# The last transposes of a stage moved among the next stage's early products, and a first stage that loads one weight piece ahead of the input

## The chip, the cores and the metric

The kernel runs on one core of a Trainium2 chip. The metric is the device time of one execution in microseconds (us). A core has a matrix engine, TensorE (PE in the profile; its weight loads are PEld), a vector engine, VectorE (DVE), a scalar engine, ScalarE (ACT), GpSimd (POOL) and SyncE (SP), which issues nearly all DMAs here. The engines run their own instruction streams and meet by semaphores.

## The reference, cut to what matters

The reference computes two blocks over 512 tokens of width 1024, in float32. `x` is (512, 1024).

```python
# block one, layer l in (0, 1); layer 0 has a dense feed-forward, layer 1 eight experts (top 2)
p = h @ w_in[l]                       # (512, 3888), then four sequence mixers on column groups
h = layer_norm(ALPHA * h + mixed @ w_out[l], ln1_g[l], ln1_b[l])
h = layer_norm(ALPHA * h + swiglu_or_experts(h), ln2_g[l], ln2_b[l])
# block two
x = x + 0.5 * rms_norm(swiglu(rms_norm(x, pre1), w_gu1, w_down1), post1)
x = x + rms_norm(hybrid_mixer(rms_norm(x, pre_mix), w_in_2, ...) @ w_o, post_mix)
x = x + 0.5 * rms_norm(swiglu(rms_norm(x, pre2), w_gu2, w_down2), post2)
```

What matters for the change: each big product needs its input feature by feature (features on the 128 partitions), while normalisation is done token by token. So between two products every tile of 128 tokens is transposed.

## The kernel before

**Products in three parts.** A float32 operand is held as two parts: a rounded one, made by ScalarE with a copy into a rounding type (`x_split` part 0, `w_split` part 0), and the rest, made by VectorE as the difference (part 1). A product is then three matmuls: rounded times rounded, and two mixed ones. `XR` (`x_split` in the profile) holds the transposed input, both parts.

**Stages.** The program is a row of stages. Each is a block in which every engine has its stream, and at whose end all engines meet; a stage starts when the last of them has arrived. Within a stage order is that of the code.

**The first stages.** `stage_load` issues the DMAs of the input (2 MB, one DMA), of four sets of constants, and of the first two weight pieces (256 columns of `w_in`, 1 MB each), and ends when the input and the constants are in. `stage_to_feature` transposes the whole input: 32 transposes of 128x128, and for each of 8 feature tiles a rounding on ScalarE and a rest on VectorE. Then `stage_stream` is the projection of layer 0: for every weight piece a rounding (1024 or 2048 elements a partition) on ScalarE, a rest on VectorE, and 48 matmuls of 512 columns on TensorE.

**Early products.** Later stages of this kind begin with a part of their first weight piece already multiplied. An `Early` object loads and splits that piece in the stage before. A `HeadStart` object runs its products for the first half of the tokens (columns 0 to 255 of `XR`) at the end of the stage before: `pe_first_tokens` waits until the piece is split and token tiles 0 and 1 are split (`moved.at(4)`), then runs 2 units (`u`) of 24 matmuls of 256 columns. `pe_last_tokens` runs the other 48 at the start of the next stage. There are four such joints: the end of `MixOut` in layer 0 (projection out of the mixers, into the dense feed-forward), the end of `LayerTail` (that feed-forward into the projection of layer 1), the end of `RootTail` (first feed-forward of block two into its projection) and the end of `OutTail`, a subclass of it (into the second feed-forward).

**The turning of a tile.** `pe_turn(t)` transposes token tile `t` in 8 transposes into two PSUM banks, `act_turned(t)` rounds them on ScalarE, and `dve_rests(t)` makes the rests on VectorE, each in two halves. The code at the end of a tail puts the early products before the last turning:

```python
if t == TT - 1 and self.start is not None:
    self.start.pe_first_tokens(self.moved.at(4), self.bank_free())
self.pe_turn(t)
```

In `RootTail` and `OutTail` the turnings run one tile later than in `LayerTail` (`behind` is 2), so that the turning of tile 2 stands in `pe_end` too. `dve_pre_norm(t)` makes the normalised rows (`h_tok`) for which `pe_turn(t)` waits.

Of the kernel before, what the change touches and what calls it, by code (L numbers as in the profile page):

```python
# [227 lines left out]
class HeadStart:  # L228
# [7 lines left out]

    def products(self, u, tokens, out=None):
        k, out = self.k, self.k.bank(self.banks[u]) if out is None else out
        for d in range(DT):
            trio = ((0, 0), (0, 1), (1, 0))  # L240
            for q, (i, j) in enumerate(trio):
                mm = self.nc.tensor.matmul(out[:, tokens], self.weights(u, i, d), k.XR[:, j, d, tokens], start=d == 0 and q == 0, stop=d == DT - 1 and q == 2)  # L242
        return mm

    def pe_first_tokens(self, split, free):
        pe = self.nc.tensor
        pe.wait_ge(*self.k.sig("early_rounded_part").at(1))
        pe.wait_ge(*self.k.sig("early_rest").at(1))
        pe.wait_ge(*split)
        pe.wait_ge(*free)  # L250
        for u in range(2):
            self.products(u, slice(0, SEQ // 2))

# [534 lines left out]
class RwkvFront(Part):  # L788
# [23 lines left out]
    def bank(self, b, n=HALF):  # L812
        return self.k.PS[:, R_PS + b * HALF:R_PS + b * HALF + n]
# [901 lines left out]
class RowTail(Part):  # L1715
# [146 lines left out]
class RootTail(RowTail):  # L1862
# [14 lines left out]
    def banks_free(self, pe):  # L1877
        pe.wait_ge(*self.first_sq.at(TT))

    def bank_free(self):  # L1880
# [79 lines left out]
    def dve_tile(self, t):  # L1960
        nc, s, k = self.nc, self.dve, self.k
        y, bank, r = k.H[:, t, :], self.scratch(t), self.col(self.r, t)
        self.dve_add(t)
        if t > 0 and self.pre:
            self.dve_new_variance(t - 1)
        nc.vector.wait_ge(*self.added.at(t + 1))
        s(nc.vector.tensor_tensor(bank, self.half(y, 1), self.half(self.gain, 1), ALU.mult))
        nc.vector.wait_ge(*self.second_sq.at(t + 1))
        nc.vector.tensor_scalar(r, self.col(self.second_sum, t), self.col(self.first_sum, t), D * RMS_EPS, ALU.add, ALU.add).then_inc(*self.var.up())
        if t > 0 and self.pre:  # L1970
            self.dve_new_factor(t - 1)
# [76 lines left out]
class MixOut(Part):  # L2048
# [160 lines left out]
    def pe_second_half(self):  # L2209
# [13 lines left out]
        if self.start is not None:  # L2223
            self.start.pe_first_tokens(self.moved.at(self.OWN + 4), self.added.at(TT + 2))
        self.pe_turn(last)
        if router is not None:
            self.pe_route(last)
# [68 lines left out]
class Kernel:  # L2296
# [386 lines left out]

    def stage_load(self, ahead):

        nc, ap = self.nc, self.ap
        loaded = self.sig("inputs_loaded")
        with nc.Block() as block:
            @block.sync
            def _(sp):  # L2690
                sp.dma_start(self.H, ap["x"][0].rearrange("(t p) d -> p t d", p=P)).then_inc(*loaded.up(16))
                sp.dma_start(self.CF[:, :], ap["const_f"]).then_inc(*loaded.up(16))
# [3 lines left out]
                ahead(sp)  # L2696
                sp.wait_ge(*loaded.at(80))

            @block.vector
            def _(dve):  # L2700
                dve.wait_ge(*loaded.at(80))
                for l in range(2):
# [3 lines left out]
        self.close()  # L2706


# [195 lines left out]
    def project(self, w, pieces, units, row, ft, tok, l=None, beside=None, start=None):  # L2904
# [11 lines left out]
        def shift(u):  # L2916
# [3 lines left out]
            return ft(u[1]), self.par(l, "mu", i), self.SM[:, OWN_MU + 9 * l + i:OWN_MU + 9 * l + i + 1]  # L2920
        self.stage_stream(w, pieces, units, HT0, copy_out, row=row, shift=shift, beside=beside, ring=PSPL if l is None else IN_RING, banks=banks, early=0 if l == 0 else 1, start=start)

# [435 lines left out]
    def block_one(self):  # L3358
        ap = self.ap
        self.stage_load(self.first_pieces(ap["w_in"][0], IN_PIECES, HT0))  # L3360
        self.stage_to_feature(self.H, None, split=self.XR)
        for l in range(2):
# [7 lines left out]
            self.project(ap["w_in"][l], IN_PIECES, IN_UNITS, rows[l * 5 + 4], self.ft, self.tok, l=l, beside=beside, start=self.piece_start() if l > 0 else None)  # L3370

# [913 lines left out]
```

## Time and profile before

| | us |
|---|---|
| median of three runs | 2974.25 |
| lowest and highest | 2971.95 and 2977.4 |
| the profiled execution | 2977.13 |
| its span in the trace | 2975.3 |

| engine | busy us | share of the span |
|---|---|---|
| PE | 2775.5 | 93% |
| PEld | 2386.3 | 80% |
| DVE | 1543.2 | 52% |
| ACT | 1086.0 | 37% |
| POOL | 208.2 | 7% |

Busy time of PE is the time in which a matmul is under way, at whichever clock. The granted clock is its second measure: 1.00 is 2.4 GHz and 0.50 is 1.2 GHz; a mean between them is a mix of the two. In a row of the timeline the first two numbers are the start and the length in us; "x48" says how many instructions are merged; the bracket says how long the engine had been idle before it and what ended that.

### The profile page before, as it was taken

The numbers are of one execution on the slowest core, as the hardware profiler recorded it, in microseconds if no ns is written. First come the engines' busy times: TensorE is split into PE (matmuls) and PEld (weight loads), VectorE is DVE, ScalarE is ACT, GpSimd is POOL, SyncE is SP. The second block draws the span as 40 slices with busy tenths as digits, with TensorE's granted clock in tenths as the row PEclk, the third lists the DMA queues.
The fourth block names the chain that finished last, engine by engine and source line by source line (L and its number), as shares of the span: only waits on it lengthen the run. The fifth ranks groups of instructions, "written<-read, shape, count | busy, mean of one in ns | idle before, by whom it ended". The sixth has DMA issues, their size and how long they took to land. (4 is left out here: it accounts for less than half of the span.)

```text
span 2975.3 us, 38798 instructions
## 1 busy us (share of the span) xinstructions
PE 2775.5 (93%) x14972; PEld 2386.3 (80%) x14972; DVE 1543.2 (52%) x2136; ACT 1086.0 (37%) x1524; POOL 208.2 (7%) x205
## 2 busy tenths in 40 slices
PE   7999999999999999969999999949999997899999
PEld 5778888888877798858988888848888775788887
DVE  3526675233355366647777777773232525742433
ACT  2434223222233242235555565532232416531222
POOL 0011200000000122050000000110000002000000
PEclk9998889999999999979999999979999996899999
DMA  4210024143222100248888888954242120251521
GB/s 152 90 62 1 29 71 124 50 138 85 85 83 90 45 1 29 86 123 235 250 237 234 228 236 235 271 144 113 60 135 85 54 64 20 85 142 50 149 69 66
DMA packets 435566, 335.25 MB, mean 113 GB/s; under 512 B 23488, under 2 KB 375744, under 8 KB 435312
## 3 DMA queue, kind: packets, MB, share of 16 engines
q1 hardware_dynamic: 429360, 318.14, 37.2%
q0 software_dynamic: 3008, 10.09, 1.0%
q10 hardware_dynamic: 3072, 5.24, 0.5%
q8 instruction: 91, 1.49, 0.2%
q14 instruction: 35, 0.29, 0.0%
HBM read 323.43 MB, written 9.99 MB: 112 GB/s over the span
## 5 line engine op out<-in xcount | busy, mean ns | idle before, releaser
L2506 PE MATMUL psum<-x_split,gate_up_split 128*128 128x512 f32 x1024 | 399.2, 390 | 2.1 <-PEq L2715 2.1
L2507 PE MATMUL psum<-x_split,gate_up_split 128*128 128x512 f32 x1024 | 399.0, 390 | 0.0
L2508 PE MATMUL psum<-x_split,gate_up_split 128*128 128x512 f32 x1024 | 398.9, 390 | 0.0
L3586 PE MATMUL psum<-x_slots_split,gate_up_split 128*128 128x320 f32 x1424 | 381.1, 346 | 16.4 <-DVE gate_up_split L3807 12.9
L3587 PE MATMUL psum<-x_slots_split,gate_up_split 128*128 128x160 f32 x1424 | 315.9, 242 | 0.0
L2634 DVE TENSOR_TENSOR arena<-arena,psum 128x512 f32<-128x512 f32 x66 | 45.4, 688 | 488.1 <-ACT arena L2572 488.1
L2847 PE MATMUL psum<-x_split,w_split 128*128 128x512 f32 x1152 | 271.9, 395 | 12.0 <-DVE w_split L2884 6.8
L3586 PEld LDWEIGHTS psum<-x_slots_split,gate_up_split 128*128 128x128 f32 x1424 | 262.6, 190 | 24.6 <-issue 22.6
L2847 PEld LDWEIGHTS psum<-x_split,w_split 128*128 128x128 f32 x1152 | 217.0, 190 | 66.6 <-issue 14.5
L3587 PEld LDWEIGHTS psum<-x_slots_split,gate_up_split 128*128 128x128 f32 x1424 | 266.1, 192 | 1.9
L2572 ACT ACTIVATE arena<-psum 128x512 f32<-128x512 f32 x66 | 39.6, 601 | 594.9 <-PE psum L2508 594.9
L2506 PEld LDWEIGHTS psum<-x_split,gate_up_split 128*128 128x128 f32 x1024 | 192.5, 188 | 42.3 <-issue 2.3
L2508 PEld LDWEIGHTS psum<-x_split,gate_up_split 128*128 128x128 f32 x1024 | 192.6, 188 | 40.1
L2507 PEld LDWEIGHTS psum<-x_split,gate_up_split 128*128 128x128 f32 x1024 | 192.6, 188 | 39.8
L3807 DVE TENSOR_TENSOR gate_up_split<-arena,gate_up_split 128x2048 fp32r<-128x2048 f32 x88 | 201.0, 2284 | 0.0
L2602 DVE TENSOR_TENSOR gate_up_split<-arena,gate_up_split 128x2048 fp32r<-128x2048 f32 x63 | 144.4, 2292 | 75.9 <-ACT gate_up_split L2553 75.9
L2525 PE MATMUL psum<-down_split,hidden_split 128*128 128x512 f32 x432 | 168.6, 390 | 1.1 <-DVE hidden_split L2636 1.1
L2526 PE MATMUL psum<-down_split,hidden_split 128*128 128x512 f32 x432 | 168.1, 389 | 0.0
L2527 PE MATMUL psum<-down_split,hidden_split 128*128 128x512 f32 x432 | 168.1, 389 | 0.0
L3740 ACT ACTIVATE gate_up_split<-arena 128x2048 fp32r<-128x2048 f32 x88 | 167.4, 1903 | 0.0
L3812 DVE TENSOR_TENSOR down_split<-arena,down_split 128x512 fp32r<-128x512 f32 x176 | 121.2, 692 | 70.6 <-ACT down_split L3746 70.0
L2847 PE MATMUL psum<-w_split,x_split 128*128 128x512 f32 (+1 forms) x672 | 143.0, 374 | 2.1 <-PE psum L2847 2.1
(520 smaller groups left out, 4790.2 us busy)
## 6 DMA issues: line engine op xcount, KB each, us to landing
arena<-in_moe_w_gate SPq DMA_DIRECT2D x91, 512.0 KB, 4.2
arena<-in_moe_w_up SPq DMA_DIRECT2D x91, 512.0 KB, 5.6
arena<-in_moe_w_down SPq DMA_DIRECT2D x176, 256.0 KB, 5.1
arena<-in_ffn_w_gu SPq DMA_DIRECT2D x88, 512.0 KB, 5.3
arena<-in_w_in SPq DMA_DIRECT2D x32, 1024.0 KB, 5.2
arena<-in_ffn_w_down SPq DMA_DIRECT2D x108, 256.0 KB, 5.2
arena<-in_ffn_w_gate SPq DMA_DIRECT2D x22, 512.0 KB, 4.1
arena<-in_ffn_w_up SPq DMA_DIRECT2D x22, 512.0 KB, 5.6
```

What stands on the lines that cost most here:

```text
L2506: nc.tensor.matmul(out, w[0], XR[:, 0, k, :], start=k == 0, stop=False)
L2507: nc.tensor.matmul(out, w[0], XR[:, 1, k, :], start=False, stop=False)
L2508: mm = nc.tensor.matmul(out, w[1], XR[:, 0, k, :], start=False, stop=k == DT - 1)
L2525: nc.tensor.matmul(out, x[0], w[0], start=f == 0, stop=False)
L2526: nc.tensor.matmul(out, x[0], w[1], start=False, stop=False)
L2527: mm = nc.tensor.matmul(out, x[1], w[0], start=False, stop=f == FU - 1)
L2602: nc.vector.tensor_tensor(GSPL[:, r, 1, :], GRAW[:, r, :], GSPL[:, r, 0, :].bitcast(F32), ALU.subtract).then_inc(*g_lo.up())
L2847: mm = nc.tensor.matmul(out, a, b, start=opens and k == 0 and q == 0, stop=closes and k == nk - 1 and q == 2)
L3586: hi = lambda start, stop: nc.tensor.matmul(out, wt[0], XE[:, k8, :, :].rearrange("p s n -> p (s n)"), start=start, stop=stop)
L3587: lo = lambda: nc.tensor.matmul(out[:, N:2 * N], wt[1], XE[:, k8, 0, :], start=False, stop=False)
L3740: nc.scalar.activation(GSPL[:, r, 0, :], GRAW[:, r, :], ACT.Copy).then_inc(g_hi.sem, 1)
L3807: nc.vector.tensor_tensor(GSPL[:, r, 1, :], GRAW[:, r, :], GSPL[:, r, 0, :].bitcast(F32), ALU.subtract).then_inc(g_lo.sem, 1)
```

## The change

It has three parts. First, the turnings at the four joints are put among the early products: in `MixOut` and `LayerTail` the last turning stands after 36 of the 48 early matmuls, in `RootTail` and `OutTail` the turnings of tiles 2 and 3 stand between the two units. Second, in `RootTail` and `OutTail` VectorE makes the rests of tile 1 before it normalises tile 2. Third, the first two stages become one, `stage_begin`, with early products for layer 0. Of the two `pe_end` below the first is that of `RowTail`, which `LayerTail` inherits, and the second is new in `RootTail`, which `OutTail` inherits.

```diff
-    def pe_first_tokens(self, split, free):
+    def pe_ready(self, split, free):
         pe = self.nc.tensor
         pe.wait_ge(*self.k.sig("early_rounded_part").at(1))
         pe.wait_ge(*self.k.sig("early_rest").at(1))
         pe.wait_ge(*split)
         pe.wait_ge(*free)
-        for u in range(2):
-            self.products(u, slice(0, SEQ // 2))
+
+    def pe_first_tokens(self, u, ds=range(DT)):
+        self.products(u, slice(0, SEQ // 2), ds)
...
     def pe_end(self):
-        for t in range(TT - self.behind, TT):
-            if t == TT - 1 and self.start is not None:
-                self.start.pe_first_tokens(self.moved.at(4), self.bank_free())
-            self.pe_turn(t)
+        start = self.start
+        start.pe_ready(self.moved.at(4), self.bank_free())
+        start.pe_first_tokens(0)
+        start.pe_first_tokens(1, range(0, DT // 2))
+        self.pe_turn(TT - 1)
+        start.pe_first_tokens(1, range(DT // 2, DT))
...
+    def pe_end(self):                       # RootTail, OutTail
+        start = self.start
+        start.pe_ready(self.moved.at(4), self.bank_free())
+        start.pe_first_tokens(0)
+        self.pe_turn(TT - 2)
+        self.pe_turn(TT - 1)
+        start.pe_first_tokens(1)
...
+        if t == TT - 1 and self.pre:
+            self.dve_rests(t - 2)
         if t > 0 and self.pre:
             self.dve_pre_norm(t - 1)
-        if t > 1 and self.pre:
+        if 1 < t < TT - 1 and self.pre:
             self.dve_rests(t - 2)
...
+    def stage_begin(self, early, start):
...
+            def _(sp):
+                sp.dma_start(self.CF[:, :], ap["const_f"]).then_inc(*const_in.up(16))
+                early.sp_load()
+                for t in range(TT):
+                    sp.dma_start(H[:, t, :], ap["x"][0, t * P:(t + 1) * P, :]).then_inc(*rows_in[t].up(16))
+                early.second(sp)
+                sp.dma_start(self.PAR[:, 0:2 * NPAR], ap["par"]).then_inc(*loaded.up(16))
+                sp.dma_start(self.MASK, ap["const_i"]).then_inc(*loaded.up(16))
+                sp.dma_start(self.B[:, NCI * P + 1024:NCI * P + 1536], ap["const_g"]).then_inc(*loaded.up(16))
+                sp.wait_ge(*loaded.at(48))
...
+            def _(pe):
...
+                pe.wait_ge(*const_in.at(16))
+                turn(0)
+                turn(1)
+                turn(2)
+                start.pe_ready(moved.at(4), moved.at(2))
+                start.pe_first_tokens(0)
+                turn(3)
+                start.pe_first_tokens(1)
...
+            def _(act):
+                early.act_round()
+                for t in range(TT):
+                    for b in range(2):
+                        act.wait_ge(*turned.at(2 * t + b + 1))
+                        nc.scalar.activation(part(0, t, b), tile(t, b), ACT.Copy).then_inc(*parts.up())
...
+            def _(dve):
+                early.dve_rest(here=True)
+                for t in range(TT):
+                    for b in range(2):
+                        dve.wait_ge(*parts.at(2 * t + b + 1))
+                        nc.vector.tensor_tensor(part(1, t, b), tile(t, b), part(0, t, b).bitcast(F32), ALU.subtract).then_inc(*moved.up())
+                dve.wait_ge(*loaded.at(48))
...
-        self.stage_load(self.first_pieces(ap["w_in"][0], IN_PIECES, HT0))
-        self.stage_to_feature(self.H, None, split=self.XR)
+        self.stage_begin(self.early_piece(ap["w_in"][0], IN_PIECES), self.piece_start())
```

On TensorE the program begins, before the change, with the transposes of the input (`h_tok`, L2725), two stage ends, and the products of the first weight pieces (L2847):

```order
L2721 UNCONDITIONAL_BRANCH
L2725 MATMUL psum<-const_sb,h_tok 128x128 x32
L2715 UNCONDITIONAL_BRANCH
L2822 UNCONDITIONAL_BRANCH
L2847 MATMUL psum<-x_split,w_split_59 128x512 x48
L2847 MATMUL psum<-x_split,w_split_60 128x512 x48
```

After the change TensorE begins with these rows; L2729 is a transpose, L241 an early product, and the rows behind the two branches belong to the projection:

```order
L2722 UNCONDITIONAL_BRANCH
L2729 MATMUL psum<-const_sb,h_tok 128x128 x24
L241 MATMUL psum<-x_split,w_split_early 128x256 x24
L2729 MATMUL psum<-const_sb,h_tok 128x128 x8
L241 MATMUL psum<-x_split,w_split_early 128x256 x24
L2709 UNCONDITIONAL_BRANCH
L2876 UNCONDITIONAL_BRANCH
L241 MATMUL psum<-x_split,w_split_early 128x256 x48
L2901 MATMUL psum<-x_split,w_split_60 128x512 x48
```

The first piece's 48 matmuls of 512 columns have become 96 of 256 columns, half of them ahead of the stage's end, and the last 8 transposes stand between them.

At the end of `MixOut` in layer 0, TensorE has before the change (L2151 are the products with `w_out`, L2194 transposes, L242 early products, L2506 the feed-forward's own):

```order
L2194 MATMUL psum<-const_sb,h_tok 128x128 x8
L242 MATMUL psum<-x_split,gate_up_split 128x256 x48
L2194 MATMUL psum<-const_sb,h_tok 128x128 x8
L2986 UNCONDITIONAL_BRANCH
L2489 UNCONDITIONAL_BRANCH
L242 MATMUL psum<-x_split,gate_up_split 128x256 x48
L2506 MATMUL psum<-x_split,gate_up_split 128x512
```

And after it, at the same place, with L2206 for the transposes and L241 for the early products:

```order
L2206 MATMUL psum<-const_sb,h_tok 128x128 x8
L241 MATMUL psum<-x_split,gate_up_split 128x256 x36
L2206 MATMUL psum<-const_sb,h_tok 128x128 x8
L241 MATMUL psum<-x_split,gate_up_split 128x256 x12
L3040 UNCONDITIONAL_BRANCH
L2505 UNCONDITIONAL_BRANCH
L241 MATMUL psum<-x_split,gate_up_split 128x256 x48
```

Twelve early products have moved behind the last turning. `LayerTail` has the same rows with `w_split_early`.

On VectorE the end of `RootTail` reads before the change as follows (L1976 adds to the residual, L1957 normalises a tile for the turning, L1803 makes the rests of a turned tile):

```order
L1976 SCALAR_TENSOR_TENSOR keep<-psum,arena,keep 128x512
L1957 SCALAR_TENSOR_TENSOR h_tok<-keep,arena 128x512 x2
L1803 TENSOR_TENSOR x_split<-psum,x_split 128x4x128 x2
L1943 TENSOR_SCALAR arena<-arena 128x1
L1948 RECIPROCAL arena<-arena 128x1
L1957 SCALAR_TENSOR_TENSOR h_tok<-keep,arena 128x512 x2
L1803 TENSOR_TENSOR x_split<-psum,x_split 128x4x128 x4
```

After the change the same instructions have the lines L1986, L1967 and L1805:

```order
L1986 SCALAR_TENSOR_TENSOR keep<-psum,arena,keep 128x512
L1805 TENSOR_TENSOR x_split<-psum,x_split 128x4x128 x2
L1967 SCALAR_TENSOR_TENSOR h_tok<-keep,arena 128x512 x2
L1953 TENSOR_SCALAR arena<-arena 128x1
L1958 RECIPROCAL arena<-arena 128x1
L1967 SCALAR_TENSOR_TENSOR h_tok<-keep,arena 128x512 x2
L1805 TENSOR_TENSOR x_split<-psum,x_split 128x4x128 x4
```

The rests of tile 1 (two instructions) now stand ahead of the normalisation of tile 2. On TensorE, 24 of the 48 early products at this place stand ahead of the turnings of tiles 2 and 3, and 24 behind.

## Rows read from the trace of the kernel before

**Rows 1.** The page: busy time of each engine, and slices of the span.

```profile
PE 2775.5 (93%) x14972; PEld 2386.3 (80%) x14972; DVE 1543.2 (52%) x2136; ACT 1086.0 (37%) x1524; POOL 208.2 (7%) x205
PE   7999999999999999969999999949999997899999
```

**Rows 2.** Timeline of the first 50 us.

```profile
1.24 0.49 SPq L2692 DMA_DIRECT2D const_sb<-in_const_f  x1
...
13.11 5.01 PE L2725 MATMUL psum<-const_sb,h_tok 128*128 128x128 f32 x32 [13.11 <-PEq L2688]
...
16.57 3.68 DVE L2744 SCALAR_TENSOR_TENSOR x_split<-psum,x_split 128x512 fp32r<-128x512 f32 x6 [0.16 <-ACT x_split L2733]
...
24.93 13.31 PE L2847 MATMUL psum<-x_split,w_split 128*128 128x512 f32 x48 [6.81 <-DVE w_split L2884]
...
38.54 11.14 PE L2847 MATMUL psum<-x_split,w_split 128*128 128x512 f32 x48 [0.30 <-PE psum L2847]
```

**Rows 3.** DMA issues of the first 20 us: count, KB each, us to landing.

```profile
h_tok<-in_x SPq DMA_DIRECT2D x1, 2048.0 KB, 7.7
arena<-in_w_in SPq DMA_DIRECT2D x2, 1024.0 KB, 13.2
const_sb<-in_const_f SPq DMA_DIRECT2D x1, 74.5 KB, 7.4
```

**Rows 4.** The page's DMA issues over the whole span.

```profile
arena<-in_w_in SPq DMA_DIRECT2D x32, 1024.0 KB, 5.2
```

**Rows 5.** Windows: stretch, its length, PE busy, granted clock, DMA share, GB/s.

```profile
2.00:8.00 6.00, 0.00 (x0) 1.00 0.98 354
8.00:12.00 4.00, 0.00 (x0) 1.00 1.03 403
```

**Rows 6.** Timeline at the end of MixOut in layer 0.

```profile
463.99 5.99 PE L242 MATMUL psum<-x_split,gate_up_split 128*128 128x256 f32 x48
...
466.54 1.42 DVE L2289 SCALAR_TENSOR_TENSOR h_tok<-h_tok,arena 128x512 f32<-128x512 f32 x2
...
469.82 1.03 PE L2194 MATMUL psum<-const_sb,h_tok 128*128 128x128 f32 x8
...
471.08 1.29 DVE L2252 TENSOR_TENSOR x_split<-psum,x_split 128x512 fp32r<-128x512 f32 x2 [1.93 <-ACT x_split L2243]
...
472.67 1.91 ACT L2553 ACTIVATE gate_up_split<-arena 128x2048 fp32r<-128x2048 f32 x1 [1.13 <-PEq L2986]
472.69 7.46 PE L242 MATMUL psum<-x_split,gate_up_split 128*128 128x256 f32 x48 [1.84 <-PEq L2986]
...
474.62 2.29 DVE L2602 TENSOR_TENSOR gate_up_split<-arena,gate_up_split 128x2048 fp32r<-128x2048 f32 x1 [2.24 <-ACT gate_up_split L2553]
```

**Rows 7.** Timeline at the end of LayerTail.

```profile
840.43 7.47 PE L242 MATMUL psum<-x_split,w_split_early 128*128 128x256 f32 x48 [1.84 <-PEq L2444]
```

**Rows 8.** Timeline at the end of RootTail.

```profile
2361.35 1.41 DVE L1957 SCALAR_TENSOR_TENSOR h_tok<-keep,arena 128x512 f32<-128x512 f32 x2
...
2362.24 1.94 PE L1784 MATMUL psum<-const_sb,h_tok 128*128 128x128 f32 x8 [3.77 <-DVE h_tok L1957]
...
2364.61 1.41 DVE L1957 SCALAR_TENSOR_TENSOR h_tok<-keep,arena 128x512 f32<-128x512 f32 x2
...
2371.54 1.04 PE L1784 MATMUL psum<-const_sb,h_tok 128*128 128x128 f32 x8
...
2374.41 5.99 PE L242 MATMUL psum<-x_split,w_split_early 128*128 128x256 f32 x48 [1.84 <-PEq L2444]
```

**Rows 9.** Timeline at the end of OutTail.

```profile
2614.22 5.99 PE L242 MATMUL psum<-x_split,gate_up_split 128*128 128x256 f32 x48 [1.84 <-PEq L4072]
```

**Rows 10.** Windows of PE alone over early products: columns as in rows 5.

```profile
472.69:480.15 7.46, 7.46 (x49) 0.77 0.93 254
2362.24:2372.58 10.34, 10.30 (x64) 0.74 0.01 2
2614.22:2620.21 5.99, 5.99 (x49) 1.00 0.87 242
```

More of the change, by code:

```diff
@@ L235, in __init__, with products @@
         self.flip = int(banks[0] == 2)
[L237 to L241, printed above, removed]
+    def products(self, u, tokens, ds=range(DT)):
+        k, out = self.k, self.k.bank(self.banks[u])
+        for d in ds:
+            for q, (i, j) in enumerate(((0, 0), (0, 1), (1, 0))):
                 mm = self.nc.tensor.matmul(out[:, tokens], self.weights(u, i, d), k.XR[:, j, d, tokens], start=d == 0 and q == 0, stop=d == DT - 1 and q == 2)
         return mm
-    def pe_first_tokens(self, split, free):
+    def pe_ready(self, split, free):
         pe = self.nc.tensor
@@ L2223, in pe_second_half @@
         if self.start is not None:
-            self.start.pe_first_tokens(self.moved.at(self.OWN + 4), self.added.at(TT + 2))
+            self.start.pe_ready(self.moved.at(self.OWN + 4), self.added.at(TT + 2))
+            self.start.pe_first_tokens(0)
+            self.start.pe_first_tokens(1, range(0, DT // 2))
         self.pe_turn(last)
+        if self.start is not None:
+            self.start.pe_first_tokens(1, range(DT // 2, DT))
         if router is not None:
@@ L2681, in tok @@
         return self.area(TOK0, TT, TOKW)[:, :, col:col + n]
-    def stage_load(self, ahead):
-        nc, ap = self.nc, self.ap
-        loaded = self.sig("inputs_loaded")
+    def stage_begin(self, early, start):
+        nc, ap, XR, H = self.nc, self.ap, self.XR, self.H
+        rows_in = [self.sig(f"x_rows_loaded{t}") for t in range(TT)]
+        const_in, loaded, turned, parts, moved = (self.sig(n) for n in ("identity_loaded", "inputs_loaded", "turned_to_feature", "feature_tile_split", "feature_tile_copied"))
+        bank = lambda t, b: self.bank(2 * t + b)
+        part = lambda i, t, b: XR[:, i, b * (DT // 2):(b + 1) * (DT // 2), t * P:(t + 1) * P]
+        tile = lambda t, b: bank(t, b).rearrange("p (k n) -> p k n", n=P)
         with nc.Block() as block:
@@ L2690, in _ @@
             def _(sp):
-                sp.dma_start(self.H, ap["x"][0].rearrange("(t p) d -> p t d", p=P)).then_inc(*loaded.up(16))
-                sp.dma_start(self.CF[:, :], ap["const_f"]).then_inc(*loaded.up(16))
+                sp.dma_start(self.CF[:, :], ap["const_f"]).then_inc(*const_in.up(16))
[3 more added lines that the diff above has]
+                early.second(sp)
                 sp.dma_start(self.PAR[:, 0:2 * NPAR], ap["par"]).then_inc(*loaded.up(16))
@@ L2695, in _, with turn @@
                 sp.dma_start(self.B[:, NCI * P + 1024:NCI * P + 1536], ap["const_g"]).then_inc(*loaded.up(16))
-                ahead(sp)
-                sp.wait_ge(*loaded.at(80))
+                sp.wait_ge(*loaded.at(48))
+            @block.tensor
+            def _(pe):
+                def turn(t):
+                    pe.wait_ge(*rows_in[t].at(16))
+                    for b in range(2):
+                        for k in range(DT // 2):
+                            d = b * (DT // 2) + k
+                            mm = nc.tensor.transpose(bank(t, b)[:, k * P:(k + 1) * P], H[:, t, d * P:(d + 1) * P], self.cf("ident"))
+                        mm.then_inc(*turned.up())
+                pe.wait_ge(*const_in.at(16))
[6 more added lines that the diff above has]
+                start.pe_first_tokens(1)
+            @block.scalar
+            def _(act):
[4 more added lines that the diff above has]
+                        nc.scalar.activation(part(0, t, b), tile(t, b), ACT.Copy).then_inc(*parts.up())
             @block.vector
             def _(dve):
-                dve.wait_ge(*loaded.at(80))
+                early.dve_rest(here=True)
+                for t in range(TT):
+                    for b in range(2):
+                        dve.wait_ge(*parts.at(2 * t + b + 1))
+                        nc.vector.tensor_tensor(part(1, t, b), tile(t, b), part(0, t, b).bitcast(F32), ALU.subtract).then_inc(*moved.up())
+                dve.wait_ge(*loaded.at(48))
                 for l in range(2):
@@ L2920, in shift @@
             return ft(u[1]), self.par(l, "mu", i), self.SM[:, OWN_MU + 9 * l + i:OWN_MU + 9 * l + i + 1]
-        self.stage_stream(w, pieces, units, HT0, copy_out, row=row, shift=shift, beside=beside, ring=PSPL if l is None else IN_RING, banks=banks, early=0 if l == 0 else 1, start=start)
+        self.stage_stream(w, pieces, units, HT0, copy_out, row=row, shift=shift, beside=beside, ring=PSPL if l is None else IN_RING, banks=banks, early=1, start=start)
     def rotary_beside(self):
@@ L3369, in beside @@
                     rotary(eng, p)
-            self.project(ap["w_in"][l], IN_PIECES, IN_UNITS, rows[l * 5 + 4], self.ft, self.tok, l=l, beside=beside, start=self.piece_start() if l > 0 else None)
+            self.project(ap["w_in"][l], IN_PIECES, IN_UNITS, rows[l * 5 + 4], self.ft, self.tok, l=l, beside=beside, start=self.piece_start())
             if l == 0:
```

## The prediction

> **What bounds the kernel now.** I read the page's busy times first: TensorE is busy for 93% of the span, and all slices but two show 7 tenths or more [rows 1]. So time can be won only where TensorE stands still, where it runs at 1.2 instead of 2.4 GHz, or where it has less to do. The change takes away almost no matmul work, so I read the timeline at the five places that it touches, and asked at each which engine arrives last.
>
> At the start TensorE does nothing until 13.11, when input and constants are in. It transposes until 18.12, and stands still again until 24.93, because the rounding and the rests of the input and then of the weight piece lie behind one another [rows 2]. Only from 24.93 on is it the bound, and every piece follows the last at once: the second begins at 38.54, 0.30 behind the end of the first.
>
> At the four joints the picture is one: the last turning stands behind all early products, and its rounding and rests come after it with nothing for TensorE beside them. In `MixOut` the turning starts at 469.82, the last rests end at 471.08 + 1.29 = 472.37, and the next stage starts at 472.69 [rows 6]. The other three joints show the same 1.84 us of idle time [rows 7 to 9].
>
> After two of these four waits the clock falls: 48 products of 256 columns take 7.46 and 7.47 us [rows 6, 7], at a mean granted clock of 0.77, while the same 48 take 5.99 in the other two places, at 1.00 [rows 8 to 10].
>
> **The start, term by term.** The constants with the identity are issued first and the weight piece second, at the 1.24 at which the second issue starts now [rows 2]. A piece of 1 MB lands 5.2 us after its issue in the median [rows 4], so at 6.4. As a cross-check, 1.1 MB at the 354 GB/s of the first stretch, from 2.0 on, are through at 5.2 [rows 5]; I take the later value. A token tile is 0.52 MB, at 403 GB/s 1.3 us [rows 5], so the four are in at 7.7, 9.0, 10.3 and 11.6. That transfers land in the order of their issue I take from the small one behind the input: issued at 1.24 and landing 7.4 later it is in at 8.6, beside the input at about 8.4 [rows 2, 3].
>
> The piece is rounded in 1.91 and its rests take 2.29 [rows 6], which gives 6.4 + 1.9 + 2.3 = 10.6. VectorE then makes four rests, 1.29 for two [rows 6], and is done at 13.2; transposes (1.03 for eight) and roundings of tiles 0 and 1 are over by then. TensorE starts 24 early products, half of 5.99 [rows 8]: 16.2. Eight transposes: 17.2. Another 24: 20.2. The constants that come last are some 1.4 MB behind 4.2 MB, in at about 18; the rests of tile 3 end at about 19. So TensorE itself is last. The next stage starts 0.3 behind the last engine's end [rows 6]; I take 0.5, since no joint here shows TensorE as the last. From 20.7 the other 48 products run until 26.7, and the second piece begins 0.30 later, at 27.0. Its own splitting, which starts with the stage, is done 4.2 us after it (474.62 + 2.29 against 472.69 [rows 6]), at 24.9, and is covered. Without that cover (a piece that lands late) it would be on the path with up to 4.2.
>
> That is 38.54 - 27.0 = 11.5 won at the full clock. Before, one spell at the low clock lies in these products: 13.31 against 11.14 for the same 48, 2.17 lost [rows 2]. TensorE stands still for about 1.5 us ahead of its first early product here, and after 1.84 it fell in two of four cases, so I charge half a spell, 1.1: **10.4**. Bounds: no spell, 11.5; two whole ones, 7.2.
>
> **The joints.** In `MixOut` the turning now starts after 36 of 48 products, at 463.99 + 0.75 x 5.83 = 468.4; the rows for it are ready at 466.54 + 1.42 = 468.0. Its rests end 2.55 after its start, at 470.9; TensorE, with the same work, is also done at 470.9 (469.82 + 1.03) [rows 6]. With 0.3 to 0.5 for the joint the next stage starts at about 471.35 instead of 472.69: 1.3 won. `LayerTail` has the same idle time [rows 7] and the same count: 1.3. Bounds for each: 1.0 and 1.5.
>
> In `RootTail` the early products wait for the rests of tile 1. These come at 2361.35, in the place of the normalisation, and end at 2362.6; before, TensorE started the turning of tile 2 at 2362.24. So it starts 0.4 later, and has the same 10.34 us of work (2362.24 to 2372.58 [rows 8, 10]): it ends at 2373.0. Behind it the tail has gone: the next start is 2373.4 instead of 2374.41, 1.0 won. What queues behind the moved rests is the normalisation of tiles 2 and 3. Tile 3 was ready at 2364.61 + 1.41 = 2366.0 [rows 8] and stays there within 0.2, while its turning now comes behind 24 products and 8 transposes, at about 2368; there is cover of some 2 us. `OutTail` is built alike: 1.1. Bounds for each: 0.2 (TensorE, at 0.74 mean clock there, gets its full clock later) and 1.4. The four joints: **4.7**, between 2.4 and 5.8.
>
> **The clock at two joints.** If an idle time of 0.4 in place of 1.84 doesn't bring the clock down, the 48 products behind `MixOut` and `LayerTail` take 5.99 instead of 7.46 and 7.47: **2.9**. Bounds: 0 and 2.9. I take the upper end, since in none of the places looked at did the clock fall without more than a microsecond of idle time ahead of it.
> The Trainium skill (TensorE: Matmul & The Clock Gate, Why this matters for your kernels) warns only of idle gaps clearly longer than the 1.84 us here. By it the falls in rows 6 and 7 would have another cause, the 2.9 would not be won, and the sum would be 15.1; two falls behind 1.84 us speak against it, two cases without a fall for it.
>
> **The sum.** 10.4 + 4.7 + 2.9 = 18.0. The profiled execution took 2977.13 and would take 2959.1. It lies 2.9 above the median of the three runs, 2974.25, so the median would be 2956.3. What follows the start is bound by TensorE and moves along; nothing else of the program is touched.
>
> **The rivals.**
> *The clock is not given back at the two joints.* For it: the clock stayed up twice behind the same idle time, so that more than the gap decides. Gain 10.4 + 4.7 = 15.1, 2959.2.
> *The transfers come late.* In one form they share the queue instead of following each other, and the piece lands as now, 13.2 after issue [rows 3], at about 15: 8.6 later than in my sum. Gain 1.8 + 4.7 + 2.9 = 9.4, 2964.9; the order of landing in rows 3 speaks against it. In the other the row tiles don't overlap. A piece's 5.2 are 2.6 beyond its bytes at 403 GB/s, so a tile would take 3.9, and the fourth be in at 6.4 + 15.6 = 22.0 instead of 11.6; turned at 23.0, with 24 products behind it, the stage ends at 26.0 instead of 20.2. Gain 18.0 - 5.8 = 12.2, 2962.1. Against it: pieces and input moved at 354 to 403 GB/s without a gap [rows 5].
> The Trainium skill (DMA: Bandwidth & Descriptors, Rules for kernel authors) wants 1 MiB or more in a DMA, and its fit has 2.0 us fixed in each. By its figures, an estimate, tiles that don't overlap would take 3.2 each, and the fourth would be in at 19.2. No row here shows transfers of this size alone in the first microseconds.
> *Nothing is won.* The piece is late, the joints give their lower bounds and the clock stays as it is: 1.8 + 2.4 = 4.2, 2970.
> *Slower.* TensorE's low clock lasts. The new first stage feeds it in small portions, with waits between tiles, and if it went on at 1.2 GHz into the projection, every microsecond there would give half a microsecond back. To turn 18.0 into a loss it needs over 36 us more at 0.50, and 48 for a loss beyond 0.2%, 2980. Before, it was back to 1.00 within the first piece (13.31 against 11.14 [rows 2]), which speaks strongly against it.
>
> **Chances and range.** The forecast 0.58, the clock not given back 0.20, late transfers 0.15, nothing won 0.05, slower 0.02. A measurement of this kernel can tell about 0.2%, 5.9 us, from no change. The first three cases lie beyond that: faster 0.93, same 0.05, slower 0.02. The likeliest case's own range is 2954 to 2959. The bounds of its terms reach down to 11.5 + 5.8 + 2.9 = 20.2, 2954, and single runs lie up to 3 from the median, so I put the low end at 2951.5; the high end, 2963.5, takes in the second case, and the late transfers but for their worst form.
>
> **What the profile after would show.** The second weight piece's first matmul at about 28, where 38.54 stood; the first early product at about 13, behind the fourth rest on VectorE, and no input tile landing later than 12. At the four joints PE idle of 0.3 to 0.6 ahead of the last-token products instead of 1.84. Behind `MixOut` and `LayerTail` 48 products in 6.0 at a clock of 1.00. My argument fails if the first early product comes after 16, if the idle times stay over 1, or if a later stage has new waits of TensorE.

## The result, and the profile after

| | us |
|---|---|
| kernel before, first series: median of 4 | 2973.1 (2966.74 to 2977.4) |
| changed kernel, first series: median of 4 | 2948.15 (2944.09 to 2950.34) |
| ratio | 0.9911, interval 0.9893 to 0.993 |
| changed kernel, the profiled execution and its span | 2949.91, 2948.1 |

The change is faster by 0.9%. Its profiled execution took 2949.91 where 2959.1 was forecast, and the median lies 8 below the forecast, and below the range. Four later series of the same kernel gave medians of 2956.83, 2956.52, 2956.88 and 2948.04. Most of this study is about that difference. One execution of the kernel before, 3104.0 at a mean clock of 0.85, stands apart from all others and is in no number below.

The page of the changed kernel: busy times, the slices of PE, and the granted clock.

```profile
PE 2761.9 (94%) x15020; PEld 2377.9 (81%) x15020; DVE 1541.0 (52%) x2136; ACT 1083.5 (37%) x1524; POOL 208.3 (7%) x205
PE   8999999999999998969999999949999996899999
...
PEclk9999989999999999879999999979999996899999
```

PE's busy time fell by 13.6 [rows 1] although it has 48 matmuls more: the same work was done at a higher mean clock. The rest of the gain is idle time.

The timeline of its start:

```profile
6.96 1.91 ACT L219 ACTIVATE w_split_early<-arena 128x2048 fp32r<-128x2048 f32 x1 [4.96 <-DMA arena<-in_w_in]
...
8.36 4.54 PE L2729 MATMUL psum<-const_sb,h_tok 128*128 128x128 f32 x24 [8.36 <-DMA h_tok<-in_x]
...
11.12 3.67 DVE L2755 TENSOR_TENSOR x_split<-psum,x_split 128x512 fp32r<-128x512 f32 x6
...
13.85 3.11 PE L241 MATMUL psum<-x_split,w_split_early 128*128 128x256 f32 x24 [0.95 <-DVE x_split L2755]
...
17.59 3.11 PE L241 MATMUL psum<-x_split,w_split_early 128*128 128x256 f32 x24
...
21.00 5.99 PE L241 MATMUL psum<-x_split,w_split_early 128*128 128x256 f32 x48 [0.30 <-PEq L2709]
...
27.29 3.89 PE L2901 MATMUL psum<-x_split,w_split 128*128 128x512 f32 x16 [0.30 <-PE psum L241]
```

The second piece begins at 27.29 where 38.54 stood [rows 2]: 11.25 won. The piece landed by 6.96, VectorE was the last to be ready (11.12 + 2.45 for four rests = 13.6), and from 13.85 on all products ran at full speed: 3.11 for 24 of them is half of 5.99, give or take the end of one.

The timeline of PE at the end of `MixOut` in layer 0, and the row of `LayerTail` that answers to [rows 7]:

```profile
450.00 4.55 PE L241 MATMUL psum<-x_split,gate_up_split 128*128 128x256 f32 x36
454.40 1.03 PE L2206 MATMUL psum<-const_sb,h_tok 128*128 128x128 f32 x8
455.19 1.68 PE L241 MATMUL psum<-x_split,gate_up_split 128*128 128x256 f32 x12
457.27 5.98 PE L241 MATMUL psum<-x_split,gate_up_split 128*128 128x256 f32 x48 [0.40 <-PEq L3040]
...
822.09 5.99 PE L241 MATMUL psum<-x_split,w_split_early 128*128 128x256 f32 x48 [0.40 <-PEq L2460]
```

From the first early product to the end of the last 13.25 pass (450.00 to 463.25) where 16.16 passed (463.99 to 480.15 [rows 6]): 2.91 won, 1.4 of it idle time and 1.48 clock. `LayerTail` is alike.

The same at the end of `RootTail`, and of `OutTail`:

```profile
2333.71 1.03 PE L1784 MATMUL psum<-const_sb,h_tok 128*128 128x128 f32 x8
2339.14 4.59 PE L241 MATMUL psum<-x_split,w_split_early 128*128 128x256 f32 x24 [4.40 <-DVE x_split L1805]
2343.58 1.91 PE L1784 MATMUL psum<-const_sb,h_tok 128*128 128x128 f32 x16
2345.24 3.11 PE L241 MATMUL psum<-x_split,w_split_early 128*128 128x256 f32 x24
2348.65 5.99 PE L241 MATMUL psum<-x_split,w_split_early 128*128 128x256 f32 x48 [0.30 <-PEq L2460]
...
2576.34 5.46 PE L241 MATMUL psum<-x_split,gate_up_split 128*128 128x256 f32 x24 [4.53 <-DVE x_split L1805]
```

The idle time behind the products has gone here too, from 1.84 to 0.30. But the wait ahead of them, 4.40 and 4.53, is longer than before (3.77 [rows 8] and 3.89), and the first 24 take 4.59 and 5.46 instead of 3.11. The rows of before in `OutTail`:

```profile
2602.69 1.69 PE L1784 MATMUL psum<-const_sb,h_tok 128*128 128x128 f32 x8 [3.89 <-DVE h_tok L1957]
2604.69 6.81 PE L242 MATMUL psum<-x_split,gate_up_split 128*128 128x256 f32 x48 [0.32 <-DVE x_split L1803]
2611.34 1.04 PE L1784 MATMUL psum<-const_sb,h_tok 128*128 128x128 f32 x8
```

**The ledger.** I took the start of the same instruction in the trace of before and in that of each profile, and noted by how much it comes earlier. The differences along the program are what each stretch gave. The changed kernel was profiled five times in all:

| stretch | first | second | third | fourth | fifth |
|---|---|---|---|---|---|
| start (touched) | 11.2 | 11.4 | 11.4 | 11.3 | 11.5 |
| mixers, layer 0 | 2.8 | 5.7 | -1.1 | 13.0 | 5.5 |
| `MixOut`'s joint (touched) | 2.9 | 2.9 | 2.9 | 2.9 | 2.9 |
| `LayerTail`'s joint (touched) | 2.9 | 2.9 | 2.9 | 2.9 | 2.9 |
| mixers, layer 1 | 5.1 | -3.0 | -5.6 | 0.5 | 0.7 |
| experts, first feed-forward of block two | -1.2 | -0.9 | -0.8 | 2.3 | 2.1 |
| `RootTail`'s joint (touched) | 2.0 | 2.0 | 2.0 | 2.0 | 2.0 |
| mixers, block two | 1.2 | -1.3 | 1.3 | 1.3 | 1.4 |
| `OutTail`'s joint (touched) | 0.3 | 1.4 | 0.2 | 0.3 | 0.3 |
| touched places, sum | 19.4 | 20.7 | 19.5 | 19.5 | 19.7 |
| untouched, sum | 7.8 | 0.5 | -6.3 | 17.0 | 9.7 |
| span | 2948.1 | 2954.1 | 2962.2 | 2938.8 | 2945.9 |

The touched places give 19.8 in the mean and hardly move. All else, in which not one instruction was changed, gives anything from -6.3 to 17.0. Its mean of 5.7 says little: the one profile of before that all are counted from took 2977.13, 3.8 above the mean of that kernel's executions, and the five profiled executions of the changed kernel lie 2.0 below its mean (both means under the fifth series).

### The profile page after: what moved, and what is told of

The parts are those of the page before. It is cut to its first block and busy times, and to the rows that moved or that the text cites. A ratio compares the mean times of both kernels' runs of the same rounds, so it can differ in the third digit from the quotient of the medians.

```text
span 2948.1 us, 38887 instructions
## 1 busy us (share of the span) xinstructions
PE 2761.9 (94%) x15020; PEld 2377.9 (81%) x15020; DVE 1541.0 (52%) x2136; ACT 1083.5 (37%) x1524; POOL 208.3 (7%) x205
## 5 line engine op out<-in xcount | busy, mean ns | idle before, releaser
L2901 PE MATMUL psum<-x_split,w_split 128*128 128x512 f32 x1104 | 258.7, 393 | 5.3 <-PE psum L2901 4.4
L2901 PEld LDWEIGHTS psum<-x_split,w_split 128*128 128x128 f32 x1104 | 206.5, 189 | 57.0 <-issue 14.4
```

The lines of the kernel that those rows point to most:

```text
L2901: mm = nc.tensor.matmul(out, a, b, start=opens and k == 0 and q == 0, stop=closes and k == nk - 1 and q == 2)
```

## The experiments

My theory after the first series, A: the touched places give 19 to 20, and what lies beyond is chance, in the clock of the mixers. The rival, B: the change moves the work behind it so that those stretches always gain some 8, and the gain is 25.

**Each part alone, and both kernels again.** The edits, cut to their main lines: `e1_begin_only` has the joints of before, `e1_joints_only` the first stages of before.

```diff
 # e1_begin_only, RowTail's pe_end (RootTail and MixOut likewise, and VectorE's order of before)
-        start.pe_first_tokens(1, range(0, DT // 2))
-        self.pe_turn(TT - 1)
-        start.pe_first_tokens(1, range(DT // 2, DT))
+                self.start.pe_first_tokens(1)
+            self.pe_turn(t)
 # e1_joints_only
-        self.stage_begin(self.early_piece(ap["w_in"][0], IN_PIECES), self.piece_start())
+        self.stage_load(self.first_pieces(ap["w_in"][0], IN_PIECES, HT0))
+        self.stage_to_feature(self.H, None, split=self.XR)
```

> The kernel before, unchanged, as a measure of the noise. Both theories: ratio 1.000 within 0.001. Theory A: its profile differs from the first one by several us in the mixers, in single steps of 1 to 2 us, while the stages bound by TensorE agree within 0.1 us. Theory B: the mixers agree with the first profile within 1 us.

Before again: 2970.2 (12 executions, 2959.22 to 2980.44), ratio to its other copy 0.9989, interval 0.9974 to 1.0003. Its profile agrees with the first one to within 0.7 in each stretch of the mixers (one step of 1.6 early in layer 0 is half given back), and the span to 0.1. That was named as the sign of B; what speaks against B comes from later profiles.

> The changed kernel once more, with more rounds. In its first profile the five places of the change brought about 19.4 us (11.2 at the start, 2.9 and 2.9 at the first two joints, 2.0 and 0.3 at the last two), and stretches that it does not touch, the mixers above all, another 8. Theory A (chance): the 8 come from where the granted clock falls in the mixers, which differs from one execution to the next; then the ratio comes out nearer 0.9935 (19 us), and in this profile the mixers' share is another one. Theory B (always there): the change brings them every time; then the ratio is again 0.991, and the mixers show 5 to 8 us again.

Changed kernel again: 2956.83 (6, 2951.49 to 2966.18), ratio 0.995, interval 0.9932 to 0.9968. The first series' 2944 to 2950 lies wholly below this one.

> The new first stage alone; all four joints as before. The second weight piece's products begin at 27.3 as in the changed kernel, 11.2 us earlier than before. Theory A: gain 11.2 us, ratio 0.9962, the mixers on average as before. Theory B: if the early start is what gives the extra time, gain 16 to 19 us, ratio 0.994 or below.

Start alone: 2961.5 (10, 2945.93 to 2978.39), ratio 0.9951, interval 0.9933 to 0.9969, so 13 won. Its profile shows the start's 11.0 in full, and a span of 2976.6, no better than before: the mixers of layer 1 had given back 8.1, `OutTail` 2.6, and the stretches between the rest.

> The four joints alone; the first two stages as before. Theory A: gain 8.1 us by the shifts read in the first profile (2.9, 2.9, 2.0, 0.3), ratio 0.9973. Theory B: if the joints give the extra time, 12 to 16 us, ratio 0.995 or below. The idle time ahead of the last-token products is 0.3 to 0.4 us at each joint, and those behind the first two joints run at a clock of 1.00.

Joints alone: 2962.39 (12, 2953.5 to 2972.6), ratio 0.9957, interval 0.9943 to 0.9971, so 12 won; in its profile the joints give 2.9, 2.9, 2.0 and 1.4, in all 9.3, and the untouched stretches the rest of 15.8.

These two series don't tell A from B. For the joints A had 8.1, which lies just outside the interval, and B's 12 lies in it; the two gains sum to more than that of the whole change. They are taken against 27 executions with a mean of 2974.3; the 12 of before again, made beside them, have 2970.5, and against those each part gives 9.

**A third series, and a filler for the waits.** The filler puts idle matmuls where TensorE waits in `RootTail` and `OutTail`, and 30 more in `MixOut`:

```diff
         start = self.start
+        self.nc.tensor.wait_ge(*self.moved.at(2))
+        for _ in range(34):
+            self.nc.tensor.matmul(self.turn_bank(2, 0)[:, 0:P], self.k.cf("ident"), self.k.cf("ident"), start=True, stop=True)
         start.pe_ready(self.moved.at(4), self.bank_free())
```

> The changed kernel a third time, for its mean over more executions and as a partner to the fillers on one chip. Theory A (chance): mean gain over all executions near 19.9 us, the sum of what its five places show in the traces, ratio 0.9933. Theory B: 25 us as in its first four executions, 0.9911.

Changed kernel, third series: 2956.52 (6, 2946.47 to 2964.66), ratio 0.9938, interval 0.9915 to 0.996. Its profile is the one with -6.3 in the untouched stretches. Windows of PE alone over the mixers of layer 1, for this profile and then for the first profile of the changed kernel, at the same work:

```profile
1100.00:1118.00 18.00, 17.08 (x157) 1.00 0.00 1
1118.00:1152.00 34.00, 34.00 (x160) 0.50 0.10 31
1152.00:1170.00 18.00, 13.08 (x98) 0.99 0.19 59
```

```profile
1114.00:1148.00 34.00, 29.59 (x239) 0.95 0.18 63
```

In one execution TensorE ran 34 us at 1.2 GHz, with 160 matmuls in them, and in the other at 2.4 GHz but for 3.4 us, with 239. One line's matmuls, of 64 columns, in the two profiles in the same order (ns: shortest, median, longest):

```profile
L1240 PE MATMUL psum<-arena x32: 314/421/421, 1122.6 to 1129.1; 128*128 128x64 f32 x32
```

```profile
L1240 PE MATMUL psum<-arena x32: 222/275/275, 1116.8 to 1120.2; 128*128 128x64 f32 x32
```

The 34 us cost 13 by the ledger. The joints alone lost 13 in the same stretch (a window of that profile shows 0.50 from 1121 to 1155), the start alone 4. B, by which these stretches always gain, is refuted: the same program gains or loses in the mixers from one execution to the next.

> The changed kernel, with idle matmuls (identity times identity, 128 columns, into a PSUM bank that is free) put where TensorE waits for 4 us ahead of the early products in RootTail and OutTail (34 of them) and ahead of the first turning in MixOut of layer 0 (30). They compute nothing that is used. Theory: the clock falls in these waits and what follows pays for it; with the fillers it stays at 1.00, and the stages behind come 1.5 to 2 us earlier at RootTail, about 1.5 at OutTail, 1.4 in MixOut: 4.5 us in all, ratio about 0.9915 if the changed kernel is at 0.993. Rival: the clock's fall there has nothing to do with these waits; then the same 48 products again take 6.8 us or more and nothing is won, or the fillers delay the products.

Filler: 2961.12 (8, 2944.14 to 2966.61), ratio 0.9951, interval 0.9925 to 0.9977. The timeline in `RootTail`:

```profile
2342.75 7.76 PE L1886 MATMUL psum<-const_sb 128*128 128x128 f32 x68
2350.26 3.11 PE L241 MATMUL psum<-x_split,w_split_early 128*128 128x256 f32 x24
```

The products behind it run at full speed, 3.11 for 24. But the filler lasts 7.76, and the rests for which the products wait were ready at 2347.07: it outlasts the wait by 3.2 and takes back more than it gives. `RootTail` gives 0.6 and `OutTail` nothing against before, instead of 2.0 and 0.3 to 1.4. The 30 in `MixOut` last 6.86, where the changed kernel waits 3.94, and of the 1.4 expected there nothing came either.

**Four variants, one execution each.** `e3_pause` adds some 1.6 us of VectorE work behind the last rests of `MixOut` and `LayerTail`:

```diff
             self.dve_tile_rests(self.last)
+            s.link(nc.vector.scalar_tensor_tensor(self.G, self.G, 1.0, self.G, ALU.mult, ALU.mult))
+            s.link(nc.vector.scalar_tensor_tensor(self.G[:, 0:256], self.G[:, 0:256], 1.0, self.G[:, 0:256], ALU.mult, ALU.mult))
```

> The changed kernel with about 1.6 us of extra VectorE work (two products of a row that nobody needs any more) behind the last rests in MixOut of layer 0 and in LayerTail, so that TensorE again stands still for nearly 2 us at these two joints, though its order is the new one. If the idle time brings the clock down, the 48 last-token products behind them take about 7.5 us again, at a clock of about 0.77. If it was the order of turning and products, they stay at 5.99.

2961.02. The timeline at `MixOut`'s joint:

```profile
451.88 1.68 PE L241 MATMUL psum<-x_split,gate_up_split 128*128 128x256 f32 x12
455.79 7.48 PE L241 MATMUL psum<-x_split,gate_up_split 128*128 128x256 f32 x48 [2.23 <-PEq L3045]
```

With 2.23 of idle time in place of 0.40, and the order of the change, the 48 products take 7.48 again; at `LayerTail` they take 7.46 behind 2.20. So it is the idle time, not the order of turning and products, that costs the clock here. With the 1.84 of before they were slow in all three profiles that have it (before, before again, start alone; both joints each), and behind 0.40 in none of twelve.

> The changed kernel with VectorE's order in RootTail and OutTail as before (tile 2 normalised, then the rests of tile 1); TensorE's order is the new one. The first early product then waits 1.4 us longer, 2364.0 against 2362.6 in the clock of the kernel before. The gain at RootTail falls from 2.0 to about 0.6 us.

Without the moved rests of tile 1 (`if t > 1 and self.pre: self.dve_rests(t - 2)`, as before), 2963.09. The wait ahead of the first early product is 5.73 instead of 4.40 and `RootTail` gives 0.7 instead of 2.0; `OutTail` -0.8 instead of 0.3. The VectorE part of the change is worth 1.1 to 1.3 at each.

> The changed kernel with the input loaded in one DMA of 2 MB behind the weight piece instead of in four. If row tiles matter, the first transpose begins at about 12.3 instead of 8.36, the first early product at about 15.6 instead of 13.85, and the second piece at about 29 instead of 27.3. If VectorE's work on the weight piece hides them, the second piece stays at 27.3.

Input in one DMA behind the piece (`sp.dma_start(H, ap["x"][0].rearrange(...))`), 2953.17. Transposes start at 11.94, the second piece at 30.51: the row tiles are worth 3.2.

> The changed kernel without early products in the first stage; loads, transposes and splitting as changed. The stage ends when the constants are in, at about 18.5; the first piece's 48 products of 512 columns follow, 11.15 us at the full clock or 13.3 with a spell at the low one. The second piece begins at 30.3 to 32.5: early products are worth 3 to 5 of the 11.2 us, order and overlap of loads and splitting the rest.

No early products in the first stage (both `start.pe_first_tokens` left out, and the first piece's 48 matmuls of 512 columns in the projection), 2958.23. The timeline of PE:

```profile
18.75 13.44 PE L2898 MATMUL psum<-x_split,w_split_early 128*128 128x512 f32 x48 [4.40 <-PEq L2709]
32.50 11.16 PE L2898 MATMUL psum<-x_split,w_split 128*128 128x512 f32 x48 [0.30 <-PE psum L2898]
```

The second piece comes 5.2 later than at 27.29: 2.3 of that is the low clock behind the longer wait (13.44 against 11.16), the rest the products that had filled the wait for the last tile.

**The order of the two loads, and a fourth series.** `e4_input_first` issues the tiles ahead of the piece (`early.sp_load()` behind the loop over the tiles).

> The changed kernel, but the four input tiles are issued ahead of the weight piece. If the order of the two loads matters as the trace of the changed kernel says (the splitting of the piece lies ahead of the first rests on VectorE, which are the last thing that the early products wait for), the piece lands at about 11.6 instead of 8.4, the first early product starts at about 17 to 18.5 instead of 13.85, and the second weight piece begins at 30.5 to 32 instead of 27.3: 3 to 4.5 lost. If the order is indifferent, because VectorE can make the rests of the first tiles before those of the piece, the second piece begins within 1 of 27.3.

2952.78 in one execution. Its start:

```profile
4.89 4.60 PE L2729 MATMUL psum<-const_sb,h_tok 128*128 128x128 f32 x24 [4.89 <-DMA h_tok<-in_x]
...
12.67 1.91 ACT L219 ACTIVATE w_split_early<-arena 128x2048 fp32r<-128x2048 f32 x1 [10.66 <-DMA arena<-in_w_in]
...
19.55 5.46 PE L241 MATMUL psum<-x_split,w_split_early 128*128 128x256 f32 x24 [10.06 <-DVE x_split L2755]
```

The second piece begins at 35.44, 8.15 later than at 27.29, twice what I expected. The piece is in at 12.67, 1.1 later than I had it, the first product comes 5.7 later, and behind 10.06 of idle time 24 products take 5.46 instead of 3.11, 2.35 more. I had left out the clock. That the whole execution took only 2952.78 says again how little a single time tells.

> The changed kernel once more, for the spread. If the first four executions were low by chance, these come around 2955 again, at a ratio of 0.993 to 0.995, and the five touched places in the profile give 19 to 20 as in the other two profiles, while the untouched stretches give anything from -8 to +8. If the gain of 25 is real and the two later series were unlucky, they come around 2948, at 0.991.

2956.88 (9, 2940.61 to 2967.39), ratio 0.9942, interval 0.9917 to 0.9967. The touched places gave 19.5 as in the others. My bound for the untouched stretches, -8 to 8, was too narrow: they gave 17.0, most of it in the mixers of layer 0. Windows of PE alone over those mixers, in this profile and in that of before:

```profile
89.00:440.00 351.00, 328.67 (x2052) 0.96 0.15 47
```

```profile
100.00:464.00 364.00, 343.52 (x2059) 0.92 0.14 45
```

**A filler of the right length, and a fifth series.** 17 idle matmuls instead of 34, none in `MixOut`.

> The changed kernel with 17 idle matmuls (half of the 34 of the longer filler) in RootTail and in OutTail, in the wait ahead of the early products, and none in MixOut. They last about 7.76 / 2 = 3.9 instead of the 4.40 and 4.53 of idle time. If the idle time is what slows the 24 early products behind it, these take 3.1 instead of 4.6 and 5.5 and start no later, RootTail gives 2.0 + 1.5 = 3.5 and OutTail 0.3 + 2.3 = 2.6 against the kernel before, and the median lies about 3.8 below that of the changed kernel. If the longer filler won nothing because the products' low clock is made up for elsewhere, the places give 2.0 and 0.3 again and the medians agree.

2946.52 (6, 2935.77 to 2954.38), ratio 0.9912, interval 0.9886 to 0.9937. The timeline in `RootTail` and, after the dots, in `OutTail`:

```profile
2323.68 3.96 PE L1886 MATMUL psum<-const_sb 128*128 128x128 f32 x34
2328.25 3.11 PE L241 MATMUL psum<-x_split,w_split_early 128*128 128x256 f32 x24 [0.61 <-DVE x_split L1805]
...
2560.46 3.96 PE L1886 MATMUL psum<-const_sb 128*128 128x128 f32 x34
2565.16 3.10 PE L241 MATMUL psum<-x_split,gate_up_split 128*128 128x256 f32 x24 [0.74 <-DVE x_split L1805]
```

`RootTail` gives 3.5 and `OutTail` 2.9 against before, instead of 2.0 and 0.3 to 1.4. So the idle time ahead of these products is what slowed them. In time the half filler is 1.5 below the changed kernel in the median and 4.5 in the mean (2944.6 against 2949.1, six executions each), which so few executions don't settle; the traces do for the two places.

> The changed kernel beside the half filler on one chip, and once more for its spread. If the 25 of the first four executions was chance, the gain over the kernel before is again 16 to 20 (the sum of the touched places is 19), and a single profile gives anything from 13 to 36; if those four show the rule, it is 25.

2948.04 (6, 2937.92 to 2961.97), ratio 0.9922, interval 0.9894 to 0.995: this series looks like the first again. Series of four to nine executions thus gave gains of 24.9, 16.1, 15.6, 18.9 and 23.6 in their means. All 31 executions of the changed kernel have a mean of 2953.7 and a standard deviation of 8.3, the 67 of before beside them 2973.3 and 5.2. The gain is 19.7, give or take 3.2 (1.96 times the root of 8.3²/31 + 5.2²/67); with the 12 of before again it would be 19.3. The touched places' 19.8 lies in that interval, B's 25 doesn't.

## Why the prediction was right and where it was wrong

**The start: right, its clock charge wrong.** Forecast 10.4, measured 11.2 to 11.5 in five profiles, where I had 11.5 for the full clock. "TensorE stands still for about 1.5 us ahead of its first early product here": it was 0.2 to 0.95, and no slow spell followed, so the term that was wrong is the half spell, charged with 1.1 and worth nothing. The piece landed by 6.96 (forecast 6.4), the first early product came at 13.85 (13.2), the next stage at 21.00 (20.7). The experiments split the gain: without the early products 5.2 less, without the row tiles 3.2 less, with the order of the loads turned round 8.2 less. The early product and the order are worth so much because of the waits that they avoid and the clock behind those waits.

**`MixOut` and `LayerTail`: right.** 1.3 + 1.5 forecast for each, 2.9 measured for each in every profile. The idle time fell from 1.84 to 0.40 and the clock stayed at 1.00; `e3_pause` shows that the one follows from the other. The rival that the clock would not be given back is refuted here. The reason given, that the clock never fell without more than a microsecond of idle time ahead of it, holds at these joints and not in the whole program: in the 13 us ahead of the 34 us above the longest idle time was 0.92.
The Trainium skill (TensorE: Matmul & The Clock Gate, Why this matters for your kernels) warns only of idle gaps clearly longer than the 1.84 us here. No run here contradicts that longer gaps cost the clock, but it is not warning enough: 1.84 us did it at these two joints, six times in six, and at the other two once in six.

**`RootTail` and `OutTail`: the sum right by luck, each term off.** Forecast 1.0 and 1.1, measured 2.0 and 0.3 (once 1.4); the two errors cancel. In `RootTail` TensorE starts 0.6 later behind its last turning, has 9.21 of work (2339.14 to 2348.35) instead of 10.34, and the joint costs 1.5 less: -0.6 + 1.1 + 1.5 = 2.0. I had said "the same 10.34 us of work"; before, the low clock had also covered a turning that took 1.94. In `OutTail` TensorE starts 0.6 later too, and the low clock lasts longer than before (5.46 + 3.12 for the 48 products, against 6.81), so that the work takes 10.32 (2576.34 to 2586.66) instead of 9.69 (2602.69 to 2612.38): -0.6 - 0.6 + 1.5 = 0.3. There the step "TensorE, at 0.74 mean clock there, gets its full clock later" was named as a bound and became the value. The half filler shows that it needn't be so.

**The sum: right; the time and the range: wrong.** The touched places were forecast at 18.0 and gave 19.8; the gain over all executions is 19.7. The steps that failed are "What follows the start is bound by TensorE and moves along; nothing else of the program is touched" and "single runs lie up to 3 from the median". TensorE does bound what follows, but at a clock that falls for 3 to 34 us at a time in the mixers, in one execution and not in the next, and that is worth -6.3 to 17.0 over the program. Three times of the kernel before, 5.5 apart, didn't show it; 67 span 27, and 31 of the changed kernel span 29. The range had to hold the median of a few executions; with a standard deviation of 8.3, the median of four to six lies some 4 off by chance (an estimate), and the range should have been about 6 wider to either side. The first series fell on the low side: theory A. The mean over 31, 2953.7, lies in the range of 2951.5 to 2963.5, and 2.6 below the forecast.

**The late transfers.** They didn't come: the piece was in by 6.96. In that rival 1.24 + 13.2 is 14.4, not 15, so its first form should have cost 8.0 and not 8.6.

**Left open.** What decides whether the clock falls in the mixers in a given execution. The records show where it fell, not why there; the idle times ahead of the 34 us above are below 1 us. Why 1.84 us cost the clock every time behind `MixOut` and `LayerTail`, and once in six behind the other two, is open as well. Whether the changed kernel's wider spread, 8.3 against 5.2, comes from the change is open too; the start alone has 8.9 (10 executions), the joints alone 5.8 (12), which would point at the start. No run moved the work behind the start by a set time and did nothing else.

## What to carry to other kernels

Count a joint twice: its idle time, and the clock of what stands behind it. At two of the four joints an idle 1.8 us cost another 1.5 at the low clock, and work that fills a wait (early products, or a filler that ends before the wait does) wins both; a filler that outlasts the wait wins nothing. Before putting a range on a time, ask how far single executions of this kernel lie apart: here the clock varies, and 31 and 67 executions left a gain of 0.7% uncertain by 3.2 us. A ledger of the touched places in two traces gave it to about 1 us from one profile of each kernel, if nothing else changes.

## What the hardware showed that I had not expected

- The order and the work unchanged, the mixers of layer 0 ended 13.0 earlier in one profile and 1.1 later in another; the granted clock over them was 0.96 in the first and 0.92 in the other.
- Idle time of 1.84 to 2.23 us was enough to bring the clock down behind `MixOut` and `LayerTail`, and not behind `RootTail`; behind `OutTail` it did in one profile (start alone, 7.48 for 48 products).
- Transfers of 512 KB queue up without a fixed cost of their own that shows: in `e4_input_first` the third tile was in by 8.40 and the fourth and the piece, 1.57 MB, by 12.67, 368 GB/s. The Trainium skill (DMA: Bandwidth & Descriptors, Rules for kernel authors) asks for 1 MiB or more in a DMA for the highest bandwidth; back to back in one queue, a transfer of half that size lost nothing that shows here.
- The small transfer of the identity, issued first and alone, landed 1.8 us after its issue, where it had taken 7.4 behind the input [rows 3].
